# Joint attention with the context's heads in pairs behind every four heads of x, gate before denominators, and per-token jobs that read PSUM directly

## The reference, cut to what matters

```python
q, k: 8 heads of 96 = 64 plain + 32 rope; k's 32 rope values are one vector per token, shared by the heads
q = rmsnorm over 96 of (cq @ w_uq), k = rmsnorm over 96 of [ckv @ w_ukv | k_rope]; rope turns the 32 of x's tokens
v: 8 heads of 64, from the same product as k
ox = softmax(qx . [kx, ky]) @ [vx, vy] * silu(ax)      # 512 queries, 768 keys
oy = softmax(qy . ky) @ vy * silu(ay)                  # 256 queries, 256 keys, layer 0 only
x = x + gate * (concat(f, g, ox) @ w_out); y likewise with oy in layer 0
```

## Time and profile before

| | us |
|---|---|
| median of 3 runs | 2487.63 (2486.51 to 2488.16) |
| profiled execution, its own time | 2488.88 |
| its span, first to last instruction | 2487.6 |
| jobs of layer 0, first ACT copy to first scores | 1878.5 to 1929.1 |
| joint attention of layer 0, first scores to first product of `tensor_out` | 1929.1 to 2060.8 |
| jobs of layer 1 | 2284.0 to 2328.3 |
| joint attention of layer 1 | 2328.3 to 2434.9 |

### The profile page before, as it was taken

The page is one execution under the profiler, slowest core; times in us unless marked ns, Lnnn a source line. Parts: engine busy times, 40 slices in busy tenths (PEclk is TensorE's granted clock), DMA queues, the critical chain, the costliest instruction groups (busy, mean ns, idle before and its releaser), DMA issues.

```text
span 2487.6 us, 31141 instructions
## 1 busy us (share of the span) xinstructions
PE 2342.9 (94%) x13278; PEld 1826.4 (73%) x13278; DVE 845.6 (34%) x1358; ACT 862.0 (35%) x1336; POOL 710.1 (29%) x309
## 2 busy tenths in 40 slices
PE   8999999999999999999989999989997989798898
PEld 6767778887888898886667777867874658685566
DVE  5644222202122323233152222035106662513662
ACT  5433223214233333333333322133226332334531
POOL 3124334445333333330343334432210002231001
PEclk9999999999999999999999999999999999899899
DMA  3122332222222212123233333222110001321001
GB/s 117 43 73 97 127 127 94 93 94 91 89 77 69 68 62 75 64 66 106 88 108 126 123 126 119 93 90 97 60 56 9 1 1 47 106 85 55 1 1 68
DMA packets 53290, 192.31 MB, mean 77 GB/s; under 512 B 6688, under 2 KB 7968, under 8 KB 52256
## 3 DMA queue, kind: packets, MB, share of 16 engines
q1 hardware_dynamic: 48960, 178.43, 21.5%
q10 hardware_dynamic: 4192, 11.90, 1.3%
HBM read 188.20 MB, written 2.10 MB: 77 GB/s over the span
## 4 chain that ended last, share of the span: by engine, by line
PE 80%; DVE 7%; ACT 2%; issue 2%; DMA 1%; DVEq 1%; ACTq 0%; POOL 0%
PE ps L182 19%; PE ps L183 18%; PE ps L184 18%; PE ps L185 3%; PE ps L187 3%; PE ps L186 3%; PE ps L2134 2%; PE ps L2160 2%; PE ps L1041 2%; PE ps L1066 2%; PE ps L2144 2%; PE ps L515 2%; PE ps L1051 1%; PE ps L1780 1%; DVE sq L2202 1%
## 5 line engine op out<-in xcount | busy, mean ns | idle before, releaser
L242 POOL TENSOR_TENSOR w_lo<-w_raw,w_hi 128x1024 fp32r<-128x1024 f32 x284 | 681.1, 2401 | 1740.1 <-ACT w_hi L176 1740.1
L182 PE MATMUL ps<-h_hi,w_hi 128*128 128x512 f32 x1168 | 479.1, 410 | 32.0 <-POOL w_lo L242 12.6
L176 ACT ACTIVATE w_hi<-w_raw 128x1024 fp32r<-128x1024 f32 x284 | 299.4, 1057 | 600.3 <-DMA w_raw<-in_wstream 599.0
L184 PE MATMUL ps<-h_hi,w_lo 128*128 128x512 f32 x1168 | 467.6, 400 | 0.0
L183 PE MATMUL ps<-h_lo,w_hi 128*128 128x512 f32 x1168 | 465.6, 399 | 0.0
L182 PEld LDWEIGHTS ps<-h_hi,w_hi 128*128 128x128 f32 x1168 | 222.0, 190 | 111.9 <-issue 31.7
L184 PEld LDWEIGHTS ps<-h_hi,w_lo 128*128 128x128 f32 x1168 | 222.0, 190 | 52.4
L183 PEld LDWEIGHTS ps<-h_lo,w_hi 128*128 128x128 f32 x1168 | 222.2, 190 | 50.5 <-issue 1.3
L1239 ACT ACTIVATE sq<-sq,dnm 128x768 f32<-128x768 f32 x64 | 59.4, 930 | 193.9 <-DVE dnm L1143 193.9
L182 PE MATMUL ps<-l_h_hi,w_hi 128*128 128x512 f32 (+3 forms) x352 | 126.1, 358 | 0.0
L184 PE MATMUL ps<-l_h_hi,w_lo 128*128 128x512 f32 (+3 forms) x352 | 124.1, 353 | 0.0
(11 more groups left out here) (285 smaller groups left out, 3942.1 us busy)
## 6 DMA issues: line engine op xcount, KB each, us to landing
w_raw<-in_wstream SPq DMA_DIRECT2D x332, 512.0 KB, 3.5
l_dft<-in_dft ACTq DMA_DIRECT2D x4, 1024.0 KB, 6.1
x<-in_x SPq DMA_DIRECT2D x4, 512.0 KB, 6.9
out<-x SPq DMA_DIRECT2D x1, 2048.0 KB, 6.3
l_wuq<-in_wuq ACTq DMA_DIRECT2D x2, 768.0 KB, 6.2
dist<-in_dist ACTq DMA_DIRECT2D x1, 1152.0 KB, 6.0
y<-in_ctx ACTq DMA_DIRECT2D x1, 1024.0 KB, 7.8
l_wukv<-in_wukv ACTq DMA_DIRECT2D x2, 512.0 KB, 3.4
```

Of the source, the lines that this page charges most:

```text
L176: self.A.activation(self.w_hi[:, n % RING, :], self.w_raw[:, n % RING, :], ACT.Copy).then_inc(self.w_high, 1)
L182: T.matmul(out, wh, ah, start=start, stop=False)
L184: return T.matmul(out, wl, ah, start=False, stop=stop)
L242: G.tensor_tensor(c.w_lo[:, n % RING, :], c.w_raw[:, n % RING, :], c.w_hi[:, n % RING, :].bitcast(F32), ALU.subtract).then_inc(c.w_low, 1)
```

## The change

In the jobs ACT no longer writes the work tile. It squares the projection where it lies in PSUM, and DVE multiplies from PSUM with one factor, root times token norm; this multiplication is what now frees the banks, together with `v_out` for v. The token's rope part of k is turned once for all heads, in the new `vector_tokens`, which stands between DVE's gate stage and its mixing stage, so that a k job has no rope work but one multiplication; its squares are added there too. In the joint attention of layer 0 a unit of context takes two heads (two scores of 256 keys side by side) and stands behind every four heads of x: 40 units in place of 48, one sequence of x and y. Sums of x go to bank 6 and of y to bank 7. The gate is multiplied first, right behind a block's last sums (step last + 3), and the denominators are inverted, spread and multiplied second, in layer 0 at a later unit of context (steps 14, 24, 29 and 34, and after the end 43 and 44, in a free bank 1 or 3), in layer 1 in the same step as the gate (10, 18, 26, 34). Sums of values now come three steps behind the scores.

```diff
 # vector_tokens, new, called between vector_in and vector_mix: DVE only
+        V.wait_ge(e.rope_in.h, self.kro0 + 1)
+        V.tensor_tensor(rt[:, 0:NT, :], kro[:, :, :], kro[:, :, :], ALU.mult)
+        V.tensor_reduce(self.skr[:, :], rt[:, 0:NT, :], AX.X, ALU.add)
...
+        V.tensor_tensor(kro[:, 0:TT, :], kro[:, 0:TT, :], rt[:, 0:TT, :], ALU.add)
+        V.tensor_tensor(self.rsq[:, :, :], c.r_tok[:, 1:3, :], c.r_tok[:, 1:3, :], ALU.mult)
+        V.tensor_scalar(self.rsq[:, 0, :], self.rsq[:, 0, :], 1.0 / A_QK, None, ALU.mult).then_inc(e.tokens_ready.h, 1)
 # tensor_heads
                     T.wait_ge(e.evacuated.h, self.ev0 + i - 1)
+                    T.wait_ge(e.v_out.h, self.vo0 + min(i - 1, NT))
 # scalar_heads
-                if what == "k":
-                    A.activation(w[:, :, A_NOPE:A_QK], self.kro[:, t, :].unsqueeze(1).broadcast_to(...), ACT.Copy)
-                    A.activation(self.vS[:, t, :], ps[:, bank + 1, :], ACT.Copy, scale=r)
-                    A.activation(w[:, :, 0:A_NOPE], heads(ps[:, bank, :]), ACT.Copy, scale=r).then_inc(e.evacuated.h, 1)
-                else:
-                    for half in range(2):
-                        ins = A.activation(flat[:, half * 384:(half + 1) * 384], ps[:, bank + half, 0:384], ACT.Copy, scale=r)
-                A.activation(wsq[i % 2], flat, ACT.Square).then_inc(e.job_squared.h, 1)
+                if what == "k":
+                    A.activation(self.wsq[i % 2][:, 0:512], self.raw(i), ACT.Square).then_inc(e.job_squared.h, 1)
+                    A.activation(self.vS[:, t, :], ps[:, (1, 3)[i % 2], :], ACT.Copy, ...).then_inc(e.v_out.h, 1)
+                else:
+                    A.activation(self.wsq[i % 2]..., self.raw(i), ACT.Square).then_inc(e.job_squared.h, 1)
 # vector_heads and finish_job
+                    V.tensor_reduce(sm, self.wsq[i % 2][:, 0:512]..., AX.X, ALU.add)
+                    V.tensor_scalar(sm, sm, self.rsq[:, 1, t:t + 1], self.skr[:, t:t + 1], ALU.mult,
+                                    ALU.add).then_inc(e.job_summed.h, 1)
         V.reciprocal(sm, sm)
-        V.tensor_tensor(w[:, :, :], w[:, :, :], sm.unsqueeze(2).broadcast_to([P, A_HEADS, A_QK]), ALU.mult)
+        V.tensor_scalar(f, sm, c.r_tok[:, 2 if what == "k" else 1, t:t + 1], None, ALU.mult)
+        if what == "k":
+            V.tensor_tensor(w[:, :, 0:A_NOPE], self.raw(i)..., f..., ALU.mult).then_inc(e.evacuated.h, 1)
+            V.tensor_tensor(w[:, :, A_NOPE:A_QK], self.kro[:, t, :]..., sm..., ALU.mult).then_inc(e.finished.h, 1)
+            return
+        for b in range(2):
+            ins = V.tensor_tensor(w[:, 4 * b:4 * b + 4, :], self.raw(i)[:, b, :]..., f[:, 4 * b:4 * b + 4]..., ALU.mult)
+        ins.then_inc(e.evacuated.h, 1)
 # Joint: units
+        for b in range(TT):
+            for half in range(2):
+                self.units += [(b, 4 * half + hd, 1) for hd in range(4)]
+                if self.both:
+                    self.units.append((TT + b // 2, 4 * (b % 2) + 2 * half, 2))
 # Joint.tensor
-            if i >= 4 and i % 2 == 0:
-                self.sum_values(i - 4)
+            if 3 <= i < self.n + 3 and i - 3 in self.of_sum:
+                self.sum_values(i - 3)
...
-            if i % 8 == 2 and i > 8:
-                self.spread_over_rows(i // 8 - 1)
+            if i in self.spreads:
+                self.spread_over_rows(*self.spreads[i])
 # Joint.vector
+            for b in range(self.blocks):
+                if i == self.last[b] + 3:
+                    self.gate_out(b)
+            if i in self.spreads:
+                self.invert(self.spreads[i][0])
+                self.norm_out(*self.spreads[i])
...
+    def gate_out(self, b):
+        V.wait_ge(e.summed_v.h, self.pv0 + self.sums[self.last[b]])
+        V.tensor_tensor(self.gt[x], c.ps[:, 6 + x, :]..., self.y.ag[:, :, self.cols(b)], ALU.mult).then_inc(e.gated.h, 1)
+    def norm_out(self, b, bank):
+        V.wait_ge(e.spread.h, self.sp0 + self.order.index(b) + 1)
+        V.tensor_tensor(gt, c.ps[:, bank, :]..., gt, ALU.mult).then_inc(e.normed.h, 1)
```

More of the change, by code:

```diff
@@ L2041, in vector @@
         self.vector_in()
+        self.vector_tokens()
         self.vector_mix()
@@ new lines, in __init__ @@
+        self.n = n = len(self.units)
+        self.exps, self.sums, self.of_sum = [], [], []
+        for i, (b, hd, heads) in enumerate(self.units):
+            self.exps.append((self.exps[-1] if i else 0) + heads)
+            ends = heads == 2 or hd % 2 == 1
+            self.sums.append((self.sums[-1] if i else 0) + ends)
+            if ends:
+                self.of_sum.append(i)
+        self.last = {b: i for i, (b, hd, heads) in enumerate(self.units)}
+        self.first = {}
+        for i, (b, hd, heads) in enumerate(self.units):
+            self.first.setdefault(b, i)
@@ new lines, in __init__ @@
+        self.spreads = {}
+        for b in range(self.blocks):
+            if not self.both:
+                self.spreads[self.last[b] + 3] = (b, 7)
+                continue
+            free = [i for i, u in enumerate(self.units) if u[2] == 2 and i >= self.last[b] + 3 and i not in self.spreads]
+            step = free[0] if free else n + 3 + (b >= TT)
+            self.spreads[step] = (b, 2 * (free[0] % 2) + 1 if free else (1, 3)[b >= TT])
+        self.order = [b for _, (b, bank) in sorted(self.spreads.items())]
@@ L2105, in keys, with width @@
+        self.tr0, self.cp0, self.pv0 = e.turned.take(n), e.copied.take(n), e.summed_v.take(self.sums[-1])
+        self.in0, self.sp0, self.ga0 = e.inverse.take(self.blocks), e.spread.take(self.blocks), e.gated.take(self.blocks)
+        self.no0, self.hi0, self.lo0 = e.normed.take(self.blocks), e.out_high.take(self.blocks), e.out_low.take(self.blocks)
     @staticmethod
-    def keys(i):
-        return (0, ALLT) if i // 8 < TT else (SEQ, CTX)
+    def width(u):
+        return ALLT if u[2] == 1 else 2 * CTX
@@ L2187, in vector @@
                 self.copy_probs(i - 2)
-            if i % 8 == 4 and i > 8:
-                self.low_out(i // 8 - 1)
+            if i - 1 in self.spreads:
+                self.low_out(self.spreads[i - 1][0])
     def max(self, i):
         c, e = self.c, self.e
+        b, hd, heads = self.units[i]
+        at = hd + A_HEADS * self.kind(b)
         c.V.wait_ge(e.scored.h, self.sc0 + i + 1)
-        c.V.tensor_reduce(self.nm[:, i % 8:i % 8 + 1], c.flat(2 * (i % 2), 0, self.keys(i)[1]), AX.X, ALU.max,
-                          negate=True).then_inc(e.maxed.h, 1)
+        scores = c.flat(2 * (i % 2), 0, self.width(self.units[i]))
@@ L2197, in copy_probs @@
+        if heads == 2:
+            scores = scores.rearrange("p (s n) -> p s n", s=2)
+        c.V.tensor_reduce(self.nm[:, at:at + heads], scores, AX.X, ALU.max, negate=True).then_inc(e.maxed.h, 1)
     def copy_probs(self, i):
-        c, e, nk = self.c, self.e, self.keys(i)[1]
+        c, e, n = self.c, self.e, self.width(self.units[i])
         c.V.wait_ge(e.turned.h, self.tr0 + i + 1)
         if i >= 3:
-            c.V.wait_ge(e.summed_v.h, self.pv0 + (i - 3) // 2 + 1)
-        c.V.tensor_copy(self.probT[i % 3][:, 0:nk], c.flat(4, 0, nk)).then_inc(e.copied.h, 1)
+            ending = next(x for x in self.of_sum if x >= i - 3)
+            c.V.wait_ge(e.summed_v.h, self.pv0 + self.sums[ending])
@@ L2237, in scalar @@
                 self.exp(i)
-            if i % 8 == 3 and i > 8:
-                self.high_out(i // 8 - 1)
+            if i in self.spreads:
+                self.high_out(self.spreads[i][0])
     def exp(self, i):
-        c, e, s, nk = self.c, self.e, i % 8, self.keys(i)[1]
+        c, e = self.c, self.e
+        b, hd, heads = self.units[i]
         c.A.wait_ge(e.maxed.h, self.mx0 + i + 1)
```

236 lines of the change are left out of this document (141 added, 95 removed).

## The result

The changed kernel took 2473.57 us (median of 5 runs, 2471.58 to 2475.34) where the kernel before took 2487.63 (5 runs): a ratio of 0.995, with a 95% interval of 0.9938 to 0.9963. Measured once more beside the experiments it took 2477.95 against 2486.49, 0.9966 (0.9951 to 0.998). One execution of the changed kernel in that second set (7094 us) and two of the kernel before (4577 and 8814 us) were slow ones; the ratio leaves them out, and without its own the changed kernel's median is 2476.24. So it is faster, by 8 to 14 us, about half a percent. The profiled execution of the first set took 2474.8, its span 2473.5. The forecast of 2473.0 lies on the result; not all of its terms do, as the stages show.

The account below looks back on a forecast made before the run. TensorE, busy for 94% of the span, was taken as the bound. Jobs -3.1 and -3.5, joint attention -1.2 and -6.8 make -14.6 us: 2488.9 to 2474.3, median 1.25 lower, 2473.0; range 2468.5 to 2480.0.

Parts of the forecast that it names:

- A: Whole kernel: the forecast itself, 2470.5 to 2476 us, chance 0.62.
- Ring of the jobs: Jobs: the VectorE and ACT chain pacing each job, k from 3.95 to 2.8 us, q from 3.95 to 4.30.
- rival F: Jobs: VectorE operands in PSUM are slow, +2.1 us, giving 2475; chance 0.02.
- ACT's table load follows v's copy ... that is inside the 3.45: Jobs' start: the 1.28 us load before the first root fits in the first interval between k sums, 3.45 us.
- The clock's +1.4 a layer: Jobs: a 3.5 us stretch at 1.2 GHz, no longer covered by VectorE, costs 1.4 us a layer, bounds 0 and 3.
- rival B: Jobs: two more stretches at 1.2 GHz per layer eat the gain, leaving -8.5 us, 2479; chance 0.15.
- Rival E: q jobs: each wait for the late bank lowers the clock, ten jobs +26 us, 2499, slower; chance 0.04.
- Joint attention, layer 0: Context stretch -24.4 us, eight added pairs +19.2, turns -4.3, end +2.2, lower clock at the end +0.5: net -6.8.
- Joint attention, layer 1: Three inner turns at 1.8 us in place of 2.6, -2.4; a worse order at the end, +1.2: net -1.2.
- "I charge nothing": Start of the joint attention: 10.2 us at half clock keep their shape, cost 0; one stretch more or less 1.7 us.
- `vector_tokens` at nothing: Ahead of mixing: some ten small VectorE operations, about 2.5 us, hidden where VectorE sits idle, cost 0.

Follow-up runs that it names:

- products at the start alone: Changed kernel plus four idle TensorE products behind the second projection of each layer's jobs: 2476.78 us, 0.9958 of the kernel before.
- all but q: Changed kernel plus inverse ahead of the gate, idle products at four places and early table loads, q still multiplied by VectorE from PSUM: 2460.5 us, 0.9891.
- products everywhere: Changed kernel plus idle TensorE products at four idle places of each layer: 2467.26 us, 0.9925 of the kernel before.
- `Joint` alone: Kernel before with only the new joint attention, jobs as before: 2481.39 us, 0.9983 of the kernel before.
- jobs alone: Changed kernel with the old joint attention, so only the jobs are new: 2485.92 us, 0.9989 of the kernel before.
- inverse first: Changed kernel with denominators inverted ahead of the gate in layer 1 and earlier at the end of layer 0: 2467.84 us, 0.9928 of the kernel before.
- and with products: Changed kernel with the inverse ahead of the gate and four idle products behind the second projection: 2466.28 us, 0.9922 of the kernel before.

## Why the prediction was right, and where it was not

- **The total** came out at 2473.57 against 2473.0, with -14.1 against -14.6. By the stages that is partly luck: of the first trace's 14.1, the changed stages gave 10.7, and 4.2 came ahead of the jobs through the clock in unchanged code, less 1.0 between the layers. By the second measurement the change gives 8.5; its 2477.95 would still lie in the range, 2468.5 to 2480.0, but not in that of A.
- **Ring of the jobs.** Forecast 2.8 for k and 4.30 for q, measured 2.85 and 4.42. Most of the 0.12 on q is the root with a scale by token, 0.30 us where it was 0.21. Multiplying from PSUM cost nothing extra, 0.69 for 512 columns (L1986) where the earlier trace rows has 0.68, so rival F falls. The rings hold where nothing disturbs them. With products at the start alone the jobs are 3.3 and 3.2 us shorter than before, where 4.5 and 4.9 were forecast without the clock; 0.75 of the gap is the table load, and 0.5 to 0.6 the 0.12 of each q interval. With all but q they are 4.6 and 4.5 us shorter, but that kernel has the table loads early, which the forecast didn't assume.
- **"ACT's table load follows v's copy ... that is inside the 3.45"** failed. Two waits precede the first root now, and the load came behind the one for the sum, 0.59 us after ScalarE fell idle. The first interval is 4.20, so 0.75 a layer is lost; with the loads early, the jobs of "all but q" are 0.9 us shorter than those with products everywhere.
- **The clock's +1.4 a layer** was the mis-sized term of the jobs: by the kernel with products at the start it was 1.0 to 2.0 us in layer 0 and 2.5 to 2.7 in layer 1. It was laid to k jobs with little slack. What brings the clock down is the third projection's wait, 4.25 and 3.62 us, for a bank that is freed late. I had counted that wait as slack. It slowed TensorE through 3.4 us in layer 0 and 6.8 in layer 1 (6.8 in both in the second trace). Jobs gave 2.4 and 0.7 in the first trace, 3.1 and 3.5 forecast. This is rival B in its mechanism (bank freed late, waits longer), at about half its price: 3.5 to 4.7 us in both layers, where B had the forecast's 2.8 and 6 more.
- **Rival E**, the clock falling in every q job, did not come: from 1890.5 to 1922.5 the granted clock is 0.97, and what is lower there is the end, from 1920.8 on. The q projections wait for their bank for 0.55 to 0.71 us, less than the 0.84 forecast. By what the Trainium skill (TensorE: Matmul & The Clock Gate, A second HAM failure mode: psum-queue depth-cycling) tells of another kernel such idles could have done it. This trace has both: no lower clock behind those short waits, and 6.8 us of it from 2043.7 on, at the end of layer 0's attention, behind waits of 1.14, 1.05, 0.80 and 1.40 us. So the skill's case is not ruled out for this kernel, but the q jobs were not the place of it.
- **Joint attention, layer 0:** forecast -6.8, measured -6.2 in the first pair of traces, -3.8 in the second and, with `Joint` alone, -4.3. The -6.2 is in part the clock at the start: the lower clock lasted 5.0 us behind the first scores, 10.2 in the kernel before and 12.5 in the second trace of the change. By those two traces of the same code a microsecond of it costs 0.41 (132.1 - 129.0 over 7.5); at the 10.2 of the kernel before I estimate the gain, from those two and from `Joint` alone, at 3.3 to 4.1 us. So the stage's own forecast was too large. The ten units from 1965.08 to 1993.22 take 28.14, which leaves 13.55 for the group without a turn; the working gave 13.5. A turn costs 1.04 and not 0.85. The end is 4.7 us and not 4.0; two spreads at the lower clock account for 0.9. These make some 1.5 us of the shortfall, and the rest is open.
- **Joint attention, layer 1:** forecast -1.2, measured -1.5 in the first trace and with `Joint` alone, -3.0 in the second pair. The turn came as forecast, a block is 24.04 us. (Its transposes were put at two thirds of 0.70, which is 0.47 and not 0.43; that is too little to see here.) The total is largely the clock again: the lower clock lasts 10.4 us behind the first scores in the kernel before, 7.7, 7.3 and 4.4 in those three. Two pairs of traces with the same `Joint` and unequal clock (before and jobs alone; inverse first, and with products) put a microsecond of it at 0.43 and 0.29, which leaves an estimated 0.2 to 1.3 us to the new order. It was not the best order: the inverse ahead of the gate is worth 0.83 a turn.
- **"I charge nothing"** for the start of the joint attention and **nothing** for the stage between the layers. The first is not right even as a difference: the stretch behind the first scores was up to 6.0 us shorter than before and up to 2.3 longer. It also hides a large reserve: filling TensorE's idle time there gave 3.2 us a layer. The second is +1.0: TensorE's 972 matmuls there take 203.4 us and not 202.3, at 0.96 and not 0.97. In the second trace the granted clock is 0.97 too, and the stage is still 1.5 longer than before: TensorE was busy for 7.2 of its 13.6 us at the lower clock, in the kernel before for 4.1 of 13.6. What counts is how much work falls into the stretch.
- **`vector_tokens` at nothing** held: the stage ahead of the jobs takes 1874.1 us in the kernel with the new jobs alone, which has it, and 1874.3 in the one with the new `Joint` alone, which doesn't.

## What to carry to other kernels

Where a buffer is freed later than before, look at how long TensorE then stands still: the wait is charged once as idle time and once more as a slower clock behind it, often in the next stage, where it hides or undoes an edit's gain. A few idle products in the wait cost nothing here, and edits that seem worth nothing alone (the table loads) show theirs once the clock holds (0.9 us in the jobs of each layer); so try them together, and judge single stages by their trace, since unchanged code alone moved by up to 10 us between traces. Compare two traces of a stage at equal time at the lower clock, or price the difference first. When an operation is put behind another on a queue, ask which of the two has its input first: the inverse here was ready before the gate and stood behind it.

## What the runs showed of the hardware that was not expected

- In the jobs, idle times of 3.6 to 4.3 us of TensorE were followed by 3.4 to 6.8 us at 1.2 GHz, in which a projection of 1.88 us took 2.90 or 3.78. With four idle products in a wait of the same length it took 1.98. One long wait was not needed: ahead of each joint attention it was two of 1.2 to 3.3 us, at the end of layer 0's four of 0.8 to 1.4.
- ScalarE's table load of 1.28 us took its place by the waits ahead of its activation: with one wait, for the sum, it ran beside VectorE's sum, with two it ran after it. The load for the exponentials stands after the first maximum in both kernels, 4.13 us after ScalarE fell idle in layer 0.
- The same matmuls ahead of the jobs, some 10225, took 1798.2 to 1807.1 us of TensorE from one trace to another.
